# Ten ring places for the first weight stream, the keys' chunks spread singly through it, and two PSUM banks by turns

## What is computed

```
sh1, sc1, g1, sh2, sc2, g2    = split(silu(c) @ w_ada + b_ada, 6)        # w_ada: 2048 x 12288, fp32
sh1c, sc1c, ...               = split(silu(c_ctx) @ w_ada + b_ada, 6)
h_l = rms_norm(x, norm1_w) * (1 + sc1) + sh1                              # x:   256 tokens x 2048
h_c = rms_norm(ctx, norm1_w) * (1 + sc1c) + sh1c                          # ctx: 256 tokens x 2048
gq, gk, gv, gr, gaf, gab, dq, dk, dv = split(h @ w_in)                    # of h_l and of h_c
```

## Time and profile before

| | us |
|---|---|
| median of 3 runs | 2486.78 (2485.66 to 2488.26) |
| the profiled execution, its own time | 2486.4 |
| its span in the trace | 2484.4 |
| PE busy / DVE busy / ACT busy | 2363.7 / 1464.6 / 1056.2 |
| SP's waits for a ring place, 0 to 215 us, released by PE / by DVE | 129.1 / 48.8 |

### The profile page before, as it was taken

The page is one execution under the profiler, slowest core; times in us unless marked ns, Lnnn a source line. Parts: engine busy times, 40 slices in busy tenths (PEclk is TensorE's granted clock), DMA queues, the critical chain, the costliest instruction groups (busy, mean ns, idle before and its releaser), DMA issues.

```text
span 2484.4 us, 37594 instructions
## 1 busy us (share of the span) xinstructions
PE 2363.7 (95%) x15615; PEld 2074.9 (84%) x15615; DVE 1464.6 (59%) x2035; ACT 1056.2 (43%) x1435; POOL 43.4 (2%) x53
## 2 busy tenths in 40 slices
PE   5779899999999998898999999999999999999997
PEld 1346787799988998778999988999978999998876
DVE  1124666649567567766888754566766543276654
ACT  3223333345456552335444433444454443254433
POOL 2000000002000000000000000000000000000000
PEclk8889999999999999999999999999999999899999
DMA  9664576645444467775877756666655566244454
GB/s 312 212 206 136 178 220 213 194 136 147 129 145 128 133 208 251 259 241 149 253 243 252 234 189 190 186 180 185 186 164 189 166 192 189 74 130 119 111 174 147
DMA packets 255433, 456.46 MB, mean 184 GB/s; under 512 B 20947, under 2 KB 49937, under 8 KB 254112
## 3 DMA queue, kind: packets, MB, share of 16 engines
q1 hardware_dynamic: 252672, 442.47, 58.0%
...
...
## 4 chain that ended last, share of the span: by engine, by line
PE 84%; DMA 5%; DVE 5%; ACT 3%; issue 1%; DVEq 1%; ACTq 0%; SPq 0%
PE psum L595 73%; DMA sbuf<-in_w_ada 2%; PE psum L662 2%; PE psum L572 2%; DVE fast L1844 2%; ACT fast L1246 1%; PE psum L1099 1%; DVE sbuf L1892 1%; DMA sbuf<-in_w_proj_diff 1%; DMA sbuf<-in_w_out 1%; PE psum L843 1%; DMA sbuf<-in_w_proj_gla 1%; PE psum L898 1%; PE psum L1129 1%; PE psum L917 1%
## 5 line engine op out<-in xcount | busy, mean ns | idle before, releaser
L595 PE MATMUL psum<-fast,fast 128*128 128x256 f32 (+3 forms) x13680 | 2084.9, 314 | 40.2 <-DVE fast L1844 32.8
L595 PEld LDWEIGHTS psum<-fast,fast 128*128 128x128 f32 (+2 forms) x13680 | 1893.0, 191 | 219.3 <-issue 47.7
L1844 DVE TENSOR_TENSOR fast<-sbuf,fast 128x1024 fp32r<-128x1024 f32 (+3 forms) x655 | 781.4, 1197 | 791.5 <-ACT fast L1246 783.7
L1246 ACT ACTIVATE fast<-sbuf 128x1024 fp32r<-128x1024 f32 (+3 forms) x659 | 678.8, 1034 | 1080.1 <-PE psum L595 918.3
L1892 DVE SCALAR_TENSOR_TENSOR sbuf<-sbuf,sbuf 128x512 f32<-128x512 f32 x240 | 180.4, 752 | 21.6 <-DMA sbuf<-in_w_ada 1.5
L1246 ACT ACTIVATE sbuf<-psum 128x512 f32<-128x512 f32 (+5 forms) x216 | 99.6, 484 | 190.0 <-PE psum L662 90.4
L662 PE MATMUL psum<-sbuf 128*32 128x512 f32 x256 | 70.6, 738 | 27.5 <-DMA sbuf<-in_w_ada 27.4
L572 PE MATMUL psum<-sbuf,sbuf 128*128 128x128 f32 (+2 forms) x317 | 56.9, 291 | 22.2 <-DMA sbuf<-in_consts 10.2
L572 PEld LDWEIGHTS psum<-sbuf,sbuf 128*128 128x128 f32 (+2 forms) x317 | 38.9, 147 | 44.6 <-issue 15.0
L662 PEld LDWEIGHTS psum<-sbuf 128*32 128x32 f32 x256 | 9.8, 118 | 69.3 <-DMA sbuf<-in_w_ada 58.4
L1864 DVE TENSOR_TENSOR fast<-sbuf,fast 128x512 fp32r<-128x512 f32 (+1 forms) x61 | 53.4, 876 | 4.6
...
## 6 DMA issues: line engine op xcount, KB each, us to landing
sbuf<-in_w_ada SPq DMA_DIRECT2D x192, 512.0 KB, 4.7
sbuf<-in_w_up SPq DMA_DIRECT2D x176, 512.0 KB, 4.0
sbuf<-in_w_in SPq DMA_DIRECT2D x158, 512.0 KB, 3.9
sbuf<-in_w_down SPq DMA_DIRECT2D x88, 512.0 KB, 4.4
sbuf<-in_w_gate SPq DMA_DIRECT2D x64, 512.0 KB, 3.7
sbuf<-in_w_out SPq DMA_DIRECT2D x64, 512.0 KB, 4.8
sbuf<-in_w_proj_gla SPq DMA_DIRECT2D x16, 512.0 KB, 4.9
sbuf<-in_w_proj_diff SPq DMA_DIRECT2D x16, 512.0 KB, 5.6
```

The source lines that it names most:

```text
L595: last = mm(out, lhsT, rhs, start=first and key not in opened, stop=end, skip_group_check=True)
L1246: return A(out, in_, ACT.Copy, scale=scale)
L1844: last = tt(lo, raw, hi.bitcast(F32), ALU.subtract)
```

## The change

1. **Ring.** While the first chunk of `ada0` to the last chunk of `gk` is issued, six more places exist, in an area that is otherwise free then (`EXTRA`). A chunk takes the place that was used longest ago (`place`), and SP waits for the release of that place's last chunk (`earlier`). In effect the ring has ten places for chunks 0 to 71 and four afterwards.
2. **Order of loads.** The chunks of `gk` come singly between those of `ada3`, `ada5` and `ada7` (`KEYS_IN`) instead of in pairs behind the panels; 6 and 7 stay last.
3. **PE's order.** `gk` chunks 0 and 1 are multiplied behind chunks 3 and 7 of `ada3`, 2 and 3 behind the same of `ada5` (`KEYS_AFTER`), 4 to 7 after `ada7`. `ada_fold(a)` moves from the end of panel a to behind chunk 1 of panel a + 1. Two token pieces are turned behind each chunk of `ada2`.
4. **Banks.** Panels 5 and 7 use banks 6 and 7 for their rows and their fold, the others 4 and 5; `rows` alternates between two buffers.
5. **ACT and DVE.** The 16 copies of turned tokens move from ACT to DVE. The four token tiles' roots are taken at once instead of two by two. The order of `rows_copy`, `round_chunk` and `modulate` on ACT and of `columns_keep`, `rest_chunk`, `gains` and `split_tokens` on DVE follows the new order of PE.

The number and shapes of all products are the same, and so is everything after `gk`.

```diff
@@ -115,6 +115,8 @@
+EXTRA = [("ada0", "gk", [5120 + SLOT_WORDS * n for n in range(6)], None)]
@@ -124,6 +126,11 @@
+KEYS_IN = {(3, 1): 0, (3, 5): 1, (5, 1): 2, (5, 5): 3, (7, 1): 4, (7, 4): 5}
+KEYS_AFTER = {(3, 3): 0, (3, 7): 1, (5, 3): 2, (5, 7): 3}
@@ -163,11 +170,11 @@
-        for q in range(4):
-            self.add(f"ada{2 * q}", ada[2 * q], 1)
-            self.add(f"ada{2 * q + 1}", ada[2 * q + 1], 1)
-            if q:
-                self.add("gk", gk[2 * q - 2:2 * q])
+        for a in range(8):
+            for i in range(8):
+                if (a, i) in KEYS_IN:
+                    self.add("gk", [gk[KEYS_IN[a, i]]])
+                self.add(f"ada{a}", [ada[a][i]], 1)
@@ -214,6 +221,19 @@
+        self.places = [(0, len(self.chunks), M_RAW + SLOT_WORDS * s, None) for s in range(SLOTS)]
+        for first, final, offsets, free in EXTRA:
+            self.places += [(self.job[first][0], self.job[final][-1] + 1, M_Y + at, free) for at in offsets]
+        self.place, self.earlier, self.loads = [], [], []
+        users = [[] for _ in self.places]
+        for g in range(len(self.chunks)):
+            s = min((n for n, (a, b, _, _) in enumerate(self.places) if a <= g < b),
+                    key=lambda n: users[n][-1] if users[n] else -1)
+            self.place.append(s)
+            self.earlier.append(users[s][-1] if users[s] else None)
+            users[s].append(g)
+            self.loads.append(len(users[s]))
@@ -254,7 +274,7 @@
-        return f"slot_loaded{g % SLOTS}", 16 * (g // SLOTS + 1)
+        return f"slot_loaded{self.place[g]}", 16 * self.loads[g]
@@ -470,8 +495,11 @@
-                if g >= SLOTS:
-                    name, count = st.released(g - SLOTS)
+                if st.earlier[g] is not None:
+                    name, count = st.released(st.earlier[g])
+                    sp.wait_ge(S(name), count)
+                elif st.places[st.place[g]][3]:
+                    name, count = st.places[st.place[g]][3]
@@ -654,12 +682,14 @@
-                if i == 0 and a:
-                    pe.wait_ge(S("ada_rows_copied"), a)
+                if a == 5 and i == 0:
+                    pe.wait_ge(S("tokens_turned"), 16)
+                elif a and i == 0:
+                    pe.wait_ge(S("ada_rows_copied"), a if a < 5 else a - 1)
...
-                    last = mm(bank(4)[32 * (k % 4):32 * (k % 4) + 32, :], csil[:, k, :], w[:, j, :], start=k < 4,
+                    last = mm(bank(rows_bank(a))[32 * (k % 4):32 * (k % 4) + 32, :], csil[:, k, :], w[:, j, :], start=k < 4,
@@ -668,13 +698,13 @@
-                sums = rows[a % 2 if a >= 8 else 0]
+                sums = rows[a % 2]
...
-                        pe.wait_ge(S("ada_kept"), a)
+                        pe.wait_ge(S("ada_kept"), a - 1 if 4 < a < 8 else a)
...
-                            last = mm(bank(5, 2 * m, 2), sums[:, m * P:(m + 1) * P], C("rowsel"), start=True, stop=True)
+                            last = mm(bank(columns_bank(a), 2 * m, 2), sums[:, m * P:(m + 1) * P], C("rowsel"), start=True, stop=True)
@@ -713,33 +743,35 @@
-            for q in range(4):
-                for a in (2 * q, 2 * q + 1):
-                    for i in range(8):
-                        ada_chunk(a, i)
-                        next(turning, None)
-                    if a == 0:
-                        pe.wait_ge(S("vectors_loaded"), 16 * NVEC_DMAS)
-                        for n in range(NVT):
-                            r = min(P, NVEC - n * P)
-                            last = transposed(bank(6 + n // 4, (n % 4) * P, r), vstage(n)[0:r, :])
-                        last.then_inc(S("vectors_turned"), 1)
-                        pe.wait_ge(S("consts_loaded"), 16)
-                        pe.wait_ge(S("lambda_products"), 1)
-                        for h in range(2):
-                            last = mm(bank(6 + h, 0, 1), C("ones")[64 * h:64 * h + 64, :],
-                                      small[64 * h:64 * h + 64, 0:1], start=True, stop=True)
-                        last.then_inc(S("lambda_summed"), 1)
-                    if a == 1:
-                        pe.wait_ge(S("lambda_done"), 1)
-                        turning = turn_tokens()
-                    ada_fold(a)
-                for j in range(2 * q - 2, 2 * q):
-                    if q:
-                        pe.wait_ge(S("h_ready"), q)
+            for a in range(8):
+                for i in range(8):
+                    ada_chunk(a, i)
+                    next(turning, None)
+                    next(turning, None)
+                    if a and i == 1:
+                        ada_fold(a - 1)
+                    if (a, i) in KEYS_AFTER:
+                        j = KEYS_AFTER[a, i]
+                        pe.wait_ge(S("h_ready"), j // 2 + 1)
...
-            for j in (6, 7):
-                pe.wait_ge(S("h_ready"), 4)
+                if a == 0:
+                    pe.wait_ge(S("vectors_loaded"), 16 * NVEC_DMAS)
+                    for n in range(NVT):
+                        r = min(P, NVEC - n * P)
+                        last = transposed(bank(6 + n // 4, (n % 4) * P, r), vstage(n)[0:r, :])
+                    last.then_inc(S("vectors_turned"), 1)
+                    pe.wait_ge(S("consts_loaded"), 16)
+                    pe.wait_ge(S("lambda_products"), 1)
+                    for h in range(2):
+                        last = mm(bank(6 + h, 0, 1), C("ones")[64 * h:64 * h + 64, :],
+                                  small[64 * h:64 * h + 64, 0:1], start=True, stop=True)
+                    last.then_inc(S("lambda_summed"), 1)
+                if a == 1:
+                    pe.wait_ge(S("lambda_done"), 1)
+                    turning = turn_tokens()
+            ada_fold(7)
+            for j in range(4, 8):
+                pe.wait_ge(S("h_ready"), j // 2 + 1)
@@ -1281,9 +1313,9 @@
-                if a:
-                    act.wait_ge(S("ada_folded"), a)
-                copy(rows[0], bank(4)).then_inc(S("ada_rows_copied"), 1)
+                if a >= 2:
+                    act.wait_ge(S("ada_folded"), a - 1)
+                copy(rows[a % 2], bank(rows_bank(a))).then_inc(S("ada_rows_copied"), 1)
@@ -1314,44 +1346,27 @@
-                if t % 2:
-                    rsqrt(small[:, 11 + t:13 + t])
+            rsqrt(small[:, 12:16])
...
-            def turned(first, last):
-                for n in range(first, last):
-                    g, t = n // 4, n % 4
-                    act.wait_ge(S("tokens_in_psum"), n + 1)
-                    copy(X[:, t // 2, 1, 4 * g:4 * g + 4, t % 2 * P:(t % 2 + 1) * P],
-                         bank(6 + n % 2).rearrange("p (a b) -> p a b", a=4)).then_inc(S("tokens_turned"), 1)
...
+                act.wait_ge(S("tokens_turned"), 4 * q + 4)
...
-            turned(0, 8)
-            act.drain()
...
-            rows_copy(2)
-            turned(8, 16)
-            act.drain()
-            rows_copy(3)
-            round_chunk(0)
-            round_chunk(1)
-            modulate(1)
-            for q in (2, 3):
-                rows_copy(2 * q)
-                rows_copy(2 * q + 1)
-                round_chunk(2 * q - 2)
-                round_chunk(2 * q - 1)
-                modulate(q)
-            for s in (6, 7):
-                round_chunk(s)
-            for s in (8, 9):
+            for a in range(2, 8):
+                rows_copy(a)
+                if a in (2, 4, 6):
+                    round_chunk(a - 2)
+                    round_chunk(a - 1)
+                else:
+                    modulate(a // 2)
+            for s in (6, 7, 8, 9):
@@ -1873,7 +1888,7 @@
-                tt(ada[:, k:k + 4, 0:n], bank(5, 0, 8).rearrange("p (a b) -> p a b", a=4)[:, :, 0:n],
+                tt(ada[:, k:k + 4, 0:n], bank(columns_bank(a), 0, 8).rearrange("p (a b) -> p a b", a=4)[:, :, 0:n],
@@ -1919,13 +1934,11 @@
-            for n in range(2):
-                dve.wait_ge(S("tokens_squared"), 2 * n + 2)
-                variance(small[:, 12 + 2 * n:14 + 2 * n], small[:, 8 + 2 * n:10 + 2 * n], D)
-                rsqrt_wait()
-                for t in (2 * n, 2 * n + 1):
-                    ts(nat[:, t, :], nat[:, t, :], small[:, 12 + t:13 + t], None, ALU.mult
-                       ).then_inc(S("tokens_scaled"), 1)
+            dve.wait_ge(S("tokens_squared"), 4)
+            variance(small[:, 12:16], small[:, 8:12], D)
+            rsqrt_wait()
+            for t in range(4):
+                ts(nat[:, t, :], nat[:, t, :], small[:, 12 + t:13 + t], None, ALU.mult).then_inc(S("tokens_scaled"), 1)
@@ -1941,14 +1954,24 @@
-            for q in range(4):
-                if q:
-                    columns_keep(2 * q)
+            def turned(first, last):
+                for n in range(first, last):
+                    g, t = n // 4, n % 4
+                    dve.wait_ge(S("tokens_in_psum"), n + 1)
+                    v.tensor_copy(X[:, t // 2, 1, 4 * g:4 * g + 4, t % 2 * P:(t % 2 + 1) * P],
```

(13 more changed lines are left out.)

7 lines of the change are left out of this document (5 added, 2 removed).

## The result

The changed kernel takes 2445.96 us (median of 4 runs, 2443.87 to 2447.42) beside 2487.52 for the kernel before on the same chip: a ratio of 0.9828 [0.9814, 0.9842]. Applied to the 2486.8 from which the prediction started, that is 2444.0, a gain of 42.8 us. The prediction said 33.9 (2453, range 2445 to 2465). The sign and the mechanism were right, the gain was a quarter larger, and the time on the prediction's own base lies 1 us under the range; with the ratio's interval it is 2440.6 to 2447.5, so the edge itself is inside the noise.

What follows compares the result with a forecast made beforehand. Four ring places were taken to bound the kernel up to 172.87 us. PE's terms from 45.2 sum to 91.9, plus 1.9 slow clock: keys 4 to 7 start at 139.0, 33.9 less, so 2486.8 becomes 2453, range 2445 to 2465.

Steps and rivals of the forecast that it cites:

- Bound before: Up to 172.87 us neither engine binds, but four places that can't hold enough for PE and loads to overlap.
- floor of loads: Loads to the last panel chunk: 1.49 us a chunk at 351 GB/s, the last landing at 121.8 us.
- `ada2`'s start: PE starts `ada2` at 45.2 us, after ACT's squares, one set of roots and the copy of bank 4.
- PE's path: PE's work and waits from 45.2 us sum to 91.9; with 1.9 of slow clock, keys 4 to 7 start at 139.0.
- waits before keys: In PE's sum, 0.4 us for a key that waits for its split by DVE.
- 48 chunks x 0.98: In PE's sum from 45.2 us, panel chunks at 0.98 us each, 47.0 us together.
- its cover the tightest: Before the third key, its split comes about 10.3 us after fold 3 where PE takes 10.6: 0.4 us of cover.
- Keys wait more than 1 us for DVE: Sign in the changed profile that the forecast is wrong, set against the cover of 0.4 us.
- rival 5: More than forecast: no slow clock or token stall, loads bind at 135, gain 38 us, 2449; below 2446 given 0.02.
- Rival 2: PE's clock stays low into `ada3`: 16 chunks more at 0.9 cost 14 us, gain 20, 2467; chance 0.07.
- "Nothing is charged": Places held by keys until DVE splits them cost nothing: 15 us or more of cover on later items.
- Rival 4: Slower than before: loads into ten places collide; at 210 GB/s 32 us later than now, 2516; chance 0.03.

Runs made afterwards that it cites:

- e1: The changed kernel with the ring's six added places taken away, four throughout, orders as changed: 2474.07 us, ratio 0.9939.
- e4: The changed kernel with eight more places where the untransposed tokens lay, from `ada4` on, eighteen in all: 2441.01 us, ratio 0.9809.
- e7: e4 with the first four keys' chunks multiplied later, behind (3,7), (4,3), (5,7) and (6,3): 2435.99 us, ratio 0.9793.
- e3: The changed kernel with all panel products going to the same two column groups instead of four: 2445.88 us, ratio 0.9825.
- e6: The changed kernel with the edits of e3 and e4 together, two column groups and eighteen places: 2444.93 us, ratio 0.9828.
- e5: The changed kernel with all panels in bank 4 and all folds in bank 5: 2447.41 us, ratio 0.9832.
- e2: The kernel before with ten places for chunks 0 to 71 and nothing else changed: 2466.75 us, ratio 0.9911.
- e9: The changed kernel, ten places, with the first four keys' chunks multiplied later as in e7: 2438.84 us, ratio 0.9812.

## Why the prediction was right in kind and short in size

**Bound before, and the floor of loads.** The bound was named rightly: with four places PE waits 32.6 us for loads (e1), with ten 11.4, and all but 1.8 of that before 33 us. The floor was not. It took a chunk at 1.49 us, from 351 GB/s. In the changed kernel the loads moved 387 GB/s from 33 to 45 us, which is 1.36 a chunk, and in long stretches of the trace the chunks land 1.36 us apart. From `ada0`'s last landing at 29.2 the 62 chunks need 84 us at that price, so the floor is 113.2 and not 121.8; e4 and e7, whose loads end at 117.7 and 118.05, lie below the forecast floor. The changed kernel ends its loads at 127.8, after 14.6 us of rests. Some 9 of these lie between 58.5 and 82.7: PE first gives back a place only each 2.0 us, a chunk and two pieces, and then come SP's two waits around key 0.

**`ada2`'s start.** Forecast 45.2, measured 44.98; the chain of squares, one set of roots and the copy was right.

**PE's path.** From 44.98 to 131.06 are 86.1 us, where the prediction had 93.8. Term by term, from the order of time and the chain of waits:

| term | forecast | measured |
|---|---|---|
| 8 chunks of `ada2` | 7.8 + 1.9 slow clock | 9.6 |
| 40 chunks of `ada3` to `ada7` | 39.2 | 27.4, with 1.8 of it a wait for a load |
| token pieces and their stall | 9.4 + 3.3 | 9.0 |
| seven folds | 7.0 | 6.7 |
| keys 0 to 3 | 22.7 | 25.9 |
| waits before keys | 0.4 | 4.9 |
| waits for ACT's copy of rows | 2.1 | 2.5 |

The step that failed is the term "48 chunks x 0.98" in the sum of PE's path. That row was a lone chunk between two pieces, and it was applied where chunks stand behind one another. The trace of before held the other price too, in rows that the prediction didn't take. PE in order of time, kernel before, four landed chunks each:

```profile
100.64 1.92 PE L662 MATMUL psum<-sbuf 128*32 128x512 f32 x16
...
144.83 1.93 PE L662 MATMUL psum<-sbuf 128*32 128x512 f32 x16
```

That is 0.48 a chunk. In the changed kernel 34 of the 40 chunks took 18.2 us, 0.54 each; the last six took 7.4, four of them as their loads came in. The term is 11.8 too high. The same price made the prediction read some 8 us of slow clock out of the 70.6 in the earlier trace rows (64 x 0.98 = 62.7); with landed chunks at half that price, more of the 70.6 was slow clock.

**What took part of it back.** Three terms were too low, and they hang together. Key 0 waited 3.07 instead of 0.4: PE came at 67.5 and not at 72.3, while DVE was ready at 70.4 (72.7 forecast). Key 2 waited 1.87: there the prediction had called its cover the tightest, and the cheap chunks used it up (its split was ready 10.8 us after fold 3, forecast 10.3). "Keys wait more than 1 us for DVE" was the prediction's own sign of an error, and it came. Behind each wait the key ran at the slow clock, 1.6 us more than the 5.7 taken. So the price of slow clock wasn't in `ada1` and `ada2` alone, where it was looked for (1.9, measured about the same), but also in two keys.

**Which of these set the end.** Not the overlap: e3, without it, starts the keys at 131.8, and e6, which hardly waits for loads, at 130.7. Even at 0.91 a chunk PE's path ends there, 8 us under the forecast. By e6's order of time that is 3.2 from chunks back to back (0.91 instead of 0.98 over 48), 0.9 from pieces in pairs (1.02 instead of 1.18 for most), 1.5 from a shorter stall, 1.4 from copies of bank 4 that are hidden behind pieces or a key before `ada3` and `ada4`, 1.9 from a clock that stays full, less 1.0 for key 0. With the overlap PE's path would end at 126.2 (e4), but with ten places the loads end at 127.8 to 129.1, and the keys start at 131.1 to 131.9. So the largest error in the sum is hidden for the most part behind the loads' end. And what shows of the gain could show only because the loads ended 7 us before the 135 that rival 5 gave them: with the 3 us that lie between the last landing and the keys in both profiles, that end gives 138. The 2453 rests on two prices that were both too high, one for PE and one for the loads.

**The clock.** Rival 2 was taken at 0.07 and didn't come: the clock fell to 0.66 from 33 to 45 us as before, and was 0.79 to 0.96 after it. Keys 0 and 2 took 7.3 us behind waits of 3.07 and 1.87, and 5.7 in e3, where key 2 doesn't wait. The wait just before isn't all of it: key 2 took 7.74 behind 0.92 in e5, where PE had stood for 2.53 us shortly before. The Trainium skill, "TensorE: Matmul & The Clock Gate", section "HAM oscillation — how this bites in real kernels", says that products in short bursts between waits for DMA start slow each time; the keys agree, though their waits were for DVE. What the prediction drew from it for the chunks doesn't agree. Arrivals each 1.36 us with 0.98 us of work between them did not keep the clock low: four such chunks of e7, from 113.94 to 118.09, took 1.05 each, and the granted clock was 1.00 from 100 to 131 us, as it was in the kernel before from 156 to 162 us.

**"Nothing is charged" for places that keys hold.** Wrong as a statement on the loads. SP stood 4.5 us for the split of key 0 and 4.3 for that of key 2, each followed by a wait (5.8 and 6.4 us) for a panel chunk that PE multiplies behind the key. The share was to stay above 0.8 and was 0.68 from 62 to 80 us. Each rest was covered when it came, since PE doesn't wait for a load between 45 and 121 us. But the rests add up to a later end of the loads, which cost PE 1.83 us at 123.27 and the slow last chunks behind it. The 48.8 us in the earlier trace rows that the prediction gave as a reason why the loads rest were mostly behind keys 4 to 7: up to 173 us they are 13.3.

**Rest of the program, and the block.** The row of 144 products was to stay 35.3 and took 33.2. Before, PE waited 1.82 us for DVE in front of it and began it at the slow level; after, it follows the fold with no wait. e2, which has that wait, has 34.77, and seven places, where the fold itself takes 1.86, 35.27; e1, with neither, 33.17. So this row too had slow clock in it, 2.1 us that the prediction left standing. The rest took 2279.0 and not 2276.3. Its code is the same in all kernels, and it took 2275.9 in e2, 2276.1 in e6, 2276.5 in e1, 2277.4 in e9, 2279.3 in e7 and 2281.8 in e4. What sets it inside these 6 us stays open; a single profiled execution of each can't tell it from chance.

**The sum.** 7.9 from PE's path, 2.1 from the block, 2.7 back: 33.9 + 7.3 = 41.2, the difference of the spans. Rival 5 had the right sign ("more than forecast"), but its bound, "the loads bind at 135", was wrong: it spaced PE's releases at 0.98 us, the same mis-sized price, and the loads at 1.49. Rival 4's time doesn't come out of its own words: 32 us later than now is 2519, not 2516; nothing rests on it.
